# A feed-forward in two halves: up projection by pairs of strips with seven products, gated strips put away in DRAM, down projection behind it

## What is computed

```python
h2 = modulate(rms_norm(x, ffn_norm_w[i]), sh_f, sc_f)
u = depthwise_conv3(h2 @ w_up[i], conv_w[i], conv_b[i])    # w_up: 1024 x 5632
gate, val = jnp.split(u, 2, axis=-1)
x = x + g_f[:, None, :] * ((jax.nn.silu(gate) * val) @ w_down[i])   # w_down: 2816 x 1024
# second block, each layer: modulation from a vector of conditions, m = silu(cond) @ w + b
```

## Time and profile before

| | us |
|---|---|
| median of 3 runs | 2347.18 (2347.07 to 2349.14) |
| the profiled execution | 2344.65, span 2342.7 |
| PE busy | 2210.0 (94%), 11436 matmuls |
| DVE busy | 1523.0 (65%) |
| ACT busy | 763.0 (33%) |
| POOL busy | 849.1 (36%) |
| mean granted clock of TensorE | 0.979 |

### The profile page before, as it was taken

How to read it: one execution, slowest core, us unless ns; L and a number is a source line. 1 busy time by engine, 2 the same in 40 slices (tenths; PEclk the granted TensorE clock), 3 DMA queues, 4 the chain that set the end, 5 groups by cost and what they waited for, 6 DMA issues and landing times. The chain is left out here.

```text
span 2342.7 us, 29053 instructions
## 1 busy us (share of the span) xinstructions
PE 2210.0 (94%) x11436; PEld 1794.2 (77%) x11436; DVE 1523.0 (65%) x2165; ACT 763.0 (33%) x995; POOL 849.1 (36%) x591
## 2 busy tenths in 40 slices
PE   5999998798999999999999999898998899999998
PEld 3887886587777788888888887587887777777876
DVE  4775506897868887766767666625997545874344
ACT  4104422587233222222222233415223333333331
POOL 0222331631426565665655221211100011688720
PEclk9999999999999999999999999899999899999999
DMA  6595722332412333433343232246346532111132
GB/s 262 198 317 167 207 75 97 121 123 65 152 54 87 116 117 97 125 113 116 116 123 107 91 126 90 81 125 173 106 139 246 189 126 108 42 54 54 54 117 81
DMA packets 125968, 290.51 MB, mean 124 GB/s; under 512 B 11974, under 2 KB 65894, under 8 KB 122728
## 3 DMA queue, kind: packets, MB, share of 16 engines
q1 hardware_dynamic: 122836, 283.55, 36.5%
q10 hardware_dynamic: 3000, 5.15, 0.6%
HBM read 237.50 MB, written 67.93 MB: 130 GB/s over the span
## 5 line engine op out<-in xcount | busy, mean ns | idle before, releaser
L3408 POOL TENSOR_TENSOR w_lo<-w_staged,w_hi 128x1024 fp32r<-128x1024 f32 x66 | 161.7, 2451 | 352.2 <-ACT w_hi L3515 352.2
L276 POOL TENSOR_TENSOR w_lo<-w_staged,w_hi 128x1024 fp32r<-128x1024 f32 x26 | 63.8, 2455 | 378.0 <-ACT w_hi L226 377.9
L2162 POOL TENSOR_TENSOR w_lo<-w_staged,w_hi 128x1024 fp32r<-128x1024 f32 x31 | 79.2, 2554 | 260.0 <-ACT w_hi L2146 260.0
L3515 ACT CAST w_hi<-w_staged 128x1024 fp32r<-128x1024 f32 x66 | 68.8, 1044 | 179.3 <-PE ps_dn L3435 178.8
L3260 DVE SCALAR_TENSOR_TENSOR ada_acc<-x_ctx,cond,ada_acc 128x512 f32<-128x512 f32 x112 | 119.8, 1100 | 2.0
L3426 PE MATMUL ps_up<-f_hi,w_hi 128*128 128x512 f32 x336 | 104.2, 391 | 5.3 <-POOL w_lo L3408 2.6
L3426 PE MATMUL ps_next<-f_hi,w_hi 128*128 128x512 f32 x336 | 107.1, 400 | 0.0
L3426 PE MATMUL ps_next<-f_lo,w_hi 128*128 128x512 f32 x336 | 103.7, 390 | 0.0
L3426 PE MATMUL ps_next<-f_hi,w_lo 128*128 128x512 f32 x336 | 103.6, 389 | 0.0
L3426 PE MATMUL ps_up<-f_lo,w_hi 128*128 128x512 f32 x336 | 103.6, 389 | 0.0
L3426 PE MATMUL ps_up<-f_hi,w_lo 128*128 128x512 f32 x336 | 103.5, 389 | 0.0
(11 more groups left out here) (678 smaller groups left out, 6211.5 us busy)
## 6 DMA issues: line engine op xcount, KB each, us to landing
w_staged<-in_w_ff SPq DMA_DIRECT2D x66, 512.0 KB, 3.7
x_ctx<-in_w_ada SPq DMA_DIRECT2D x48, 512.0 KB, 5.2
x_in<-in_w_ada SPq DMA_DIRECT2D x16, 1024.0 KB, 8.1
scratch_bias<-scratch_line SPq DMA_DIRECT2D x32, 512.0 KB, 7.8
att_bias<-scratch_bias SPq DMA_DIRECT2D x32, 512.0 KB, 3.3
w_staged<-in_w_in SPq DMA_DIRECT2D x17, 512.0 KB, 5.5
ada_w<-in_w_ada SPq DMA_DIRECT2D x8, 1024.0 KB, 19.9
w_staged<-in_w_v SPq DMA_DIRECT2D x16, 512.0 KB, 3.5
```

The lines of the kernel that those rows point to most:

```text
L276: nc.gpsimd.tensor_tensor(st.lo[i % 2][:, 0:widths[i]], st.staged[i % 2][:, 0:widths[i]], st.hi[i % 2][:, 0:widths[i]].bitcast(F32), ALU.s ...
L2162: nc.gpsimd.tensor_tensor(st.lo[i % 2][:, :], st.staged[i % 2][:, :], st.hi[i % 2][:, :].bitcast(F32), ALU.subtract).then_inc(st.split, 1)
L3408: nc.gpsimd.tensor_tensor(st.lo[i % 2][:, :], st.staged[i % 2][:, :], st.hi[i % 2][:, :].bitcast(F32), ALU.subtract).then_inc(st.split, 1)
L3515: nc.scalar.copy(st.hi[i % 2][:, :], st.staged[i % 2][:, :]).then_inc(st.hi_ready, 1)
```

## The change

The feed-forward is cut in two.

First half: strips of j = 0 and 1 as before; then x is put away to DRAM, T1 to T4 are formed (`SplitHalvesKept`, `PairInputs`), and j = 2 to 21 are made as 20 pairs, gate and value strip of one j together, by a class `UpPairs`. It differs from `StripPairs` in that results are summed in place in PSUM, with two sets of four banks used in turn, and in who makes the rests: POOL those of products 0, 3, 4 and 5, VectorE those of 1, 2 and 6. Centring, taps, Silu and the merge of j - 1 run beside pair j. The merged (gated) strip is stored to DRAM. POOL makes B' in this half (`mats.ahead`, five instructions of 384 columns a pair), and SP stores it.

Second half: the down projection in 11 chunks of two j. Each chunk's gated strips and weights are loaded (`load_chunk`), split by ACT and VectorE, and each of 8 output tiles gets 12 matmuls, so VectorE adds 88 times to x where it added 176 times. Every fifth tile is followed by a turn of B' (loaded back) and the next by the taps; the taps are made for 32 rows a group and stored by 24 DMAs for a group of three instead of 8, six behind each of four tiles.

`SecondAda` becomes `BothAda` (4 pieces, both conditions, in the first half) and `LateAda` (8 pieces, in the project of u: a batch of 11 VectorE steps after each strip is taken out). `SplitAhead` runs in the second half.

```diff
+    def high(self, act, q, m):           # UpPairs
+        if m in self.SUMS:
+            act.wait_ge(self.summed, 4 * q + self.SUMS[m])
+        if self.count(q, m) > 4:
+            act.wait_ge(self.multiplied, self.count(q, m) - (2 if self.closing(q, m) else 4))
...
+    def product(self, pe, q, m):
+        place, (high, low) = self.place(q, self.PLACES[m]), self.inputs[m]
+        self.wait_low(pe, q, m)
+        if m == 2:
+            pe.wait_ge(self.copied, q + 1)
+        if m == 3:
+            pe.wait_ge(self.added, 5 * q + 1)
+        if m == 5:
+            pe.wait_ge(self.added, 5 * q + 2)
+        if m == 6:
+            pe.wait_ge(self.added, 5 * q + 3)
...
+            def load_chunk(c):
+                for j in (2 * c, 2 * c + 1):
+                    load_a(j, both_loaded[(j - 2) % 4])
+                    load_w(j)
...
+            store_a(LASTJ)
+            for u in mats.finished(N):
+                mats.store_bp(sp, u)
+            sp.wait_ge(ada.weighted, ada.STEPS * ada.PIECES)
+            mats.all_bp_stored(sp)
+            mats.load_bp(sp, 0)
...
+                for part in range(mats.PARTS):
+                    if n - 3 - part in TURN_AT:
+                        sp.wait_ge(down, n)
+                        mats.store_taps(sp, TURN_AT.index(n - 3 - part), part)
...
+            for q in range(N):               # TensorE
+                j = q + pairs.FIRST
+                for m in range(pairs.PRODUCTS):
+                    if q == 0:
+                        inputs.wait(pe, m)
+                    if m == 0:
+                        pe.wait_ge(merged, j - 1)
...
+                    pairs.product(pe, q, m)
+                    if m == 4 and q in ADD_AT:
+                        pe.wait_ge(tapped, 4 * (j - 1) + 2)
+                        ada.add_up(pe, ADD_AT[q], pairs.value(j - 1))
...
+                    pairs.second_block(dve, q - 1)      # VectorE, pair q
+                    taps(j - 1, 1)
+                    taps(j - 1, 0)
+                    pairs.second_sum(dve, q)
+                    merge(j - 1)
+                    pairs.dve_low(dve, q, 6)
+                    ada_steps(q, (0,))
+                    pairs.third_sum(dve, q)
+                ada_steps(q, (1, 2))
+                pairs.last_block(dve, q)
...
+                ada_steps(q, (3,))
...
+                pairs.third_block(dve, q)
+                if q + 1 < N:
+                    pairs.dve_low(dve, q + 1, 1)
+                    pairs.dve_low(dve, q + 1, 2)
...
+            if ada is not None:              # project, TensorE
+                ada.tensor(pe, 1)
```

More of the change, by code:

```diff
@@ L202, in _ @@
                     begin()
+                if ada is not None:
+                    for p in ada.BEFORE_PUT.get(i, ()):
+                        ada.load(sp, p)
                 if store is not None and 2 <= i < n:
@@ L3342, in gated_ffn @@
+def gated_ffn(nc, g, st, x, hi, lo, raw, rounded, mixed, before, inputs, ps, pairs, ada, mats, ahead, context, into, early, late, spilled, back):
+    base, loads, taken = st.strips, tuple(st.loads), st.taken
+    N, LASTJ = pairs.N, KF - 1
+    CHUNKS = KF // 2
+    STRIPS = KD * CHUNKS
+    TURN_AT = [3 + 5 * b for b in range(mats.N)]
+    ADD_AT = {4 * p + 5: p for p in range(ada.PIECES)}
+    CONTEXT = 3
     gate_f = g.mod[:, G_F:G_F + KD, 0]
-    ONES = g.ones[:, 0:1].to_broadcast([P, D])
+    places, window = (ps[0], ps[1], ps[2]), ps[3][:, :]
+    t_gate, t_val = mixed[:, 0, :], mixed[:, 1, :]
+    stored_a = nc.dram_tensor("scratch_ff_a", (KF, P, L), F32).ap()
@@ L3398, in _ @@
             mats.all_stored(sp)
             early.all_stored(sp)
+            for p in range(2):
+                late.load(sp, p)
             into.spill(sp)
@@ new lines, in high, with pair_high @@
+                if i < 4:
+                    act.wait_ge(st.done, base + i - 1)
+                else:
+                    act.wait_ge(down, KD)
+                nc.scalar.copy(st.hi[i % 2][:, :], st.staged[i % 2][:, :]).then_inc(st.hi_ready, 1)
+            def pair_high(q, m):
+                if m in (0, 5):
+                    act.wait_ge(st.loaded[m // 5], loads[m // 5] + 16 * (q + 3))
+                if q == 0 and m < 4:
+                    act.wait_ge(st.done, base + 3 + m // 2)
+                pairs.high(act, q, m)
@@ new lines, in centre @@
+            def centre(j, which):
+                t, source = (t_val, pairs.value(j)) if which else (t_gate, pairs.gate(j))
+                col = j + which * KF
+                if j < 2:
+                    act.wait_ge(st.done, base + 2 * j + which + 1)
+                else:
+                    act.wait_ge(pairs.added, 5 * (j - 2) + (4 if which else 5))
+                if j == 0:
+                    act.wait_ge(inputs.formed, inputs.T3_FORMED)
+                elif which:
+                    act.wait_ge(a_stored, 16 * j)
+                else:
+                    act.wait_ge(silued, j)
+                at = VEC["conv_b"] + col
+                nc.scalar.activation(t, source[:, :], ACT.Identity, scale=tap(1, col), bias=g.vecs[:, at:at + 1]).then_inc(centred, 1)
@@ new lines, in build @@
+            t3 = (block(flat(rounded, 0)), block(flat(rounded_third, 0)), block(piece(0, 4)))
+            four_done = st.strips + 4
+            inputs = PairInputs(nc, g, ctx, "ff_in", norm, t1, t2, t3, hi, lo, lambda engine: engine.wait_ge(st.done, four_done))
+            pairs = UpPairs(nc, st, ctx, inputs.products(), ps, [piece(4 + i) for i in range(3)], piece(7), piece(8), piece(9))
+            after = InverseRms(nc, g, nm, ctx, "n3", x, KD, L, None, ps_n2, [piece(0, 2), piece(2, 2)], piece(4, 2), cols_3, halved=True)
@@ L4496, in build @@
+            mats = StepMatrices(nc, g, ctx, row(2, 2), piece(10, 3), piece(9), par)
+            spilled = g.middle("ff_x_spilled")
+            back = [g.middle(f"ff_x_back{s}") for s in range(2)]
+            gated_ffn(nc, g, st, x, hi, lo, raw, rounded, mixed, norm, inputs, ps, pairs, ada, mats, [g.dram["w_u"][i] for i in range(2)], context,
                       IntoBlockTwo(nc, g, ctx, x[:, :, :], after, rms_4, squares_4, x_spilled),
-                      SplitAhead(nc, g, ctx, [par[:, i * L:(i + 1) * L] for i in range(4)], mats))
+                      SplitAhead(nc, g, ctx, [piece(2 * i, 2) for i in range(4)]), late, spilled, back)
```

1072 lines of the change are left out of this document (708 added, 364 removed).

## The result

The changed kernel takes 2322.89 us (median of 4 runs, 2321.3 to 2323.95) where the kernel before took 2347.12 in the same comparison: ratio 0.9899, 95% interval 0.9882 to 0.9916, 1.0% faster. I had forecast 2298. The time lies inside the range, but the gain is 24 us and not 49: half of what was forecast is missing.

A forecast was written before the change was run, and what follows sets the result against it. The feed-forward was taken as bound by TensorE's count of matmuls. -54.4 + 10.7 + 2.2 - 6.0 - 1.7 = -49.2 us, from the median 2347.18 to 2298 us; range 2283 to 2324.

The forecast's parts named there:

- The count of matmuls: Feed-forward, 20 pairs: 84 matmuls each where 96 stood, 240 fewer at 0.2267 us, -54.4 us.
- The loop of a pair: First half: a 16.98 us chain over ACT, POOL and VectorE delays product 3 by 0.66 in 16 pairs, +10.7 us.
- Rival (b): Pairs: VectorE's two rests each wait 0.65 us longer on the lock with POOL; 2311 to 2324 us, chance 0.18.
- The start: First four strips of the feed-forward and the forming of T1 to T4: 9.6 us over matmuls where 7.4 stood, +2.2 us.
- part 6: SP's issue of 24 small tap DMAs instead of 8: under 100% busy, 0 us, with 20 us as the other end.
- Rival (c): Second half: small stores cost SP 0.6 us each, it falls 3 us behind per chunk; 2318 us, chance 0.09.
- part 4: Gaps and second half: old waits go, new ones come, turns and taps cost the same; -6.0 us in all.
- the first turn: Start of the second half: TensorE waits 4.6 us for B' to be loaded back.
- The modulation: Half its sums stay beside the pairs, half go to the project of u with one 0.9 us wait; -1.7 us.
- part 5: The modulation's term; six of eight 2 MB loads in u add some 200 GB/s, just hidden, up to 5 us otherwise.
- signs of being wrong: A pair over 21 us, TensorE waiting at strips 8c for rests, or SP with no gap left.
- part 3: The feed-forward's start: 7.8 us over four strips as in the odd mixer, plus 1.7 for a Silu; +2.2 us.

The follow-up runs named there:

- e2_sum_first: The changed kernel with VectorE's second sum moved ahead of the gate taps: 2314.59 us, ratio 0.9867 to the kernel before.
- e3_few_steps: The changed kernel with 56 of the 64 modulation steps on VectorE beside the pairs left out: 2308.97 us, a single run.
- e6_ahead_early: The changed kernel with POOL's two products for B' moved ahead of its subtraction and sums: 2312.0 us, ratio 0.9853 to the kernel before.
- e1_taps3: The changed kernel with the taps of a group of three stored by 3 DMAs instead of 24: 2300.42 us, ratio 0.9808 to the kernel before.
- e9_taps12: The changed kernel with taps stored by 12 DMAs of two lags each instead of 24: 2307.19 us, ratio 0.9816 to the kernel before.
- e12_stores_late: e8_all with SP storing the later project's split strip at a chunk's fourth tile, in seven of eight cases, not at its start: 2287.27 us.
- e8_all: The changed kernel with 3 tap DMAs, second sum and block earlier, SP's new order at the change of halves, POOL's B' products earlier: 2288.41 us.

## Why the prediction was right and wrong

**The count of matmuls** was right: 240 fewer at 0.2267 us.

**The loop of a pair** was right in its mechanism and, by luck, in size: 17.01 to 17.19 us for 16.98, a pair with steps 19.85 for 19.7, those behind sums 19.04, the release of product 3 by the second sum, which e2_sum_first shows, and the modulation steps as what lengthens it, which e3_few_steps shows. Two terms missed and cancelled: POOL's subtraction and sums with ACT's start took 7.51 us, where I had 8.15; the rests took 2.41 to 2.59, where I had 1.75, "at 0.94 less overlap". That was a row of a VectorE instruction beside POOL part of the time; here POOL never stops. The +5.8 us are 0.3 in pair 0 and 1.3 in pair 1 (counting from 0), where the work of the start is still behind; 0.17 in each of nine pairs; 0.3 in each of three with sums; 1.1 in pair 17, to which I gave no steps though the last ones lie in its loop; 0.35 in the last; and 0.4 of rounding.

VectorE's rest takes 1.24 and 1.50 us beside POOL and 0.68 with POOL idle (the rows of the pair and of e6_ahead_early), while its tap with PSUM takes 1.27 as in the earlier trace rows. With the rule of the Trainium skill that I had weighed (SBUF — State Buffer, Who interferes with whom: two SBUF inputs on VectorE share a lock with POOL) the runs agree. Rival (b) priced it at 0.65 for each rest; it was 0.33 to 0.42 each against my value, and the subtraction gave most of it back.

**The start** took 49.9 us and not 53.1. The Silu that I had priced at 1.7 us is in the chain (VectorE waits 1.97 for it ahead of the product, which ends at 733.35), but TensorE's strips last until 733.3 and product 0 starts at 733.40, so it costs TensorE 0.1. And of the odd mixer's 7.8 over the matmuls only 6.4 came, this 0.1 included: the first two strips took 27.87 us, as there, the two behind them 22.0 where they took 23.5.

**The second half** was wrong, by 22.6 us, and the step that failed is part 6, the 0 us for SP; e1_taps3 measures 19.3. Its arithmetic held: 24 issues of 0.45 and seven others in 15.5 us is 88%, and SP's rows cover 85%. The conclusion "under 100%, and its loads are wanted late: 0 us" did not. The loads are wanted late only if they are issued when they may be; behind up to 24 stores of another job they come up to 11 us later, and B' and C', which are one deep (a load waits for the turn before, POOL for the store of the C' before), have no such slack. e1_taps3 gives 19.3 us back by taking stores away, e9_taps12 shows that the loss goes with their number and doesn't begin at 100%. Rival (c) named the right engine, and its sum (20 us, 2318) came out by luck: its mechanism was a queue over 100% that falls further behind with each chunk, from issues of 0.6 us; an issue took 0.42 us in the median, near the 0.437 of the earlier trace rows, and the queue was not that full. I gave it 0.09 because I looked only at whether the queue fills up.

**The gaps of part 4**: the first turn was right to half a microsecond (4.35 by the starts for 4.6), the last pair too (2.18 for 2.1). With SP out of the way the second half is 286.8 for my 283.4, but that is luck again. Part 4 has the taps "cost the same": 22.6 us; they took 9.3. Against these 13.3 us, waits of 26.8 stand where I had 12.3: 4.6 ahead of turns (4.1 of them the first) and 8.1 ahead of strips, as about forecast, and then 9.0 ahead of taps, 2.7 behind turns and taps and 2.3 ahead of the context's sums, for which I had no term. For one of the waits at taps e12_stores_late shows the cause, SP's own wait; for the others it stays open.

**The modulation** in the project of u: 98.3 us for 98.0, with one wait of 1.31 after the second strip where I had 0.9. The 2 MB loads held VectorE (4.0 us once, 1.1 to 1.8 three times) and never TensorE. They brought this stretch from 127 to 245 GB/s, 118 on top and not the "some 200" of part 5.

**The range** held the time at its upper end, with (b) and (c) as its bounds. The pairs cost 5.8 us more than forecast and SP 19.3. That the time stayed inside is partly luck: without the 13.3 us that the taps saved it would be 2336, an estimate that counts all of them. Of the signs of being wrong, waits for rests at strips 8c came (1.1, 2.2, 0.5 and 1.7 us at strips 8, 32, 48 and 72), within the 6.5 us counted for them.

**Slips in the working.** 16 x 0.66 is 10.6 and not 10.7, part 3's 7.8 and 1.7 add up to 9.5 and not 9.6, and the four terms named leave 20.4 of the 73.6 us, where part 4 takes off 19.9. Together they move the forecast by under a microsecond.

## What to carry to other kernels

- An in-order queue of DMA issues is not free below 100% (8.2 us lost at 70%, 19.3 at 85%). For each transfer that something waits for soon, count what stands in front of it in the queue at the moment it becomes possible, and what the queue itself may be waiting for; the mean load says nothing about that. Moving issues to another engine moves the delay to what that engine does next.
- Where many small DMAs store windows of one tile, one DMA with an overlapping pattern may do: 24 became 3.
- A stretch that takes as long as forecast can hold two errors that cancel. Here the taps were 13.3 us cheaper and the waits 14.5 us longer than forecast; only adding up each kind by itself showed it.
- A loop over several engines is found by following one buffer once round. When it is a few tenths too long, look first for an engine that can do its side work where it idles, and expect that shortening one link shows the next one.

## What the hardware showed that I had not expected

- What a DMA costs the queue is nearly independent of its size (a load of 512 KB took 0.38 us of SP in the row at 1317.33), and a pattern of several overlapping windows costs a little more than a plain one: a store of one lag took SP 0.420 us in the median, of two 0.592, of eight 0.566 (ns, least, median and most, of the change, of e9_taps12 and of e1_taps3):

```profile
L3157 SPq DMA_DIRECT2D scratch_toeplitz<-ff_room x384: 302/420/2312, 1163.2 to 1438.6; - x192
```

```profile
L3159 SPq DMA_DIRECT2D scratch_toeplitz<-ff_room x192: 559/592/1687, 1161.0 to 1419.2; - x192
```

```profile
L3159 SPq DMA_DIRECT2D scratch_toeplitz<-ff_room x48: 559/566/1433, 1160.6 to 1407.2; - x48
```

- VectorE's subtraction of 128x512 in SBUF took 0.68 us alone and 1.24 to 1.50 beside POOL, POOL's 1.29 alone and up to 1.75.
- 24 matmuls of 64 rows by 128 columns took TensorE 1.41 us when all of them wrote the same rows of PSUM, and 0.58 when each three wrote rows 32 apart: six at once instead of two.
- The stretch of sums and norms between the stage and u holds the same instructions in every kernel made from the change and took 39.5 to 45.9 us, at granted clocks of 0.87 (e2_sum_first) to 0.74 (the four kernels with SP's new order, 45.9 each). TensorE does short matmuls and waits there; what decides when its clock falls, these runs don't settle. It hides or feigns gains of some 3 us in a comparison of totals. The work ahead of the pairs does the same, by up to 3.4 us: from 300 to 600 us, where the work is the same, the granted clock was 0.94 in the change and 0.96 in e8_all.
